# The low half of every fourth feed-forward weight group: ScalarE's negated high half and an accumulating transfer in place of VectorE's subtraction

## The reference

```python
hn = rmsnorm(x, norm_ffn_pre[l])
u = jnp.square(jax.nn.relu(jnp.einsum('bsd,df->bsf', hn, w_up[l])))     # w_up   2048 x 8192
y = jnp.einsum('bsf,fd->bsd', u, w_down[l])                             # w_down 8192 x 2048
x = x + rmsnorm(y, norm_ffn_post[l])
```

## Time and profile before

| | us |
|---|---|
| median of 3 runs | 2577.0 (2576.7 to 2577.39) |
| the profiled execution, its own time | 2578.93 |
| its span in the trace | 2577.2 |
| TensorE busy | 2571.3 (100%) |
| VectorE busy | 1582.6 (61%) |
| ScalarE busy | 1246.6 (48%) |
| GpSimd busy | 34.8 (1%) |

### The profile page before, as it was taken

The page is one execution under the profiler, slowest core; times in us unless marked ns, Lnnn a source line. Parts: engine busy times, 40 slices in busy tenths (PEclk is TensorE's granted clock), DMA queues, the critical chain, the costliest instruction groups (busy, mean ns, idle before and its releaser), DMA issues.

```text
span 2577.2 us, 29181 instructions
## 1 busy us (share of the span) xinstructions
PE 2571.3 (100%) x11503; PEld 2131.7 (83%) x11503; DVE 1582.6 (61%) x1842; ACT 1246.6 (48%) x1495; POOL 34.8 (1%) x56
## 2 busy tenths in 40 slices
PE   9999999999999999999999999999999999999999
PEld 7888888888888888888888888888888888888887
DVE  5646565566666566676866876556575555555555
ACT  6554443444555555455544444444464354454453
POOL 1000000000000000000000000000010000000000
PEclk9999999999999999999999999999999999999999
DMA  8767766676777777777565877666566676676674
GB/s 273 205 193 208 205 205 192 199 205 199 216 217 198 211 207 199 223 224 218 168 187 167 222 215 216 203 200 197 192 212 215 194 202 218 186 217 208 196 223 151
DMA packets 534793, 527.41 MB, mean 205 GB/s; under 512 B 294896, under 2 KB 297824, under 8 KB 534656
## 3 DMA queue, kind: packets, MB, share of 16 engines
q1 hardware_dynamic: 531856, 518.09, 67.5%
q0 software_dynamic: 2384, 6.93, 1.1%
q10 hardware_dynamic: 416, 0.52, 0.1%
HBM read 488.24 MB, written 2.10 MB: 190 GB/s over the span
## 4 chain that ended last, share of the span: by engine, by line
PE 99%; DMA 0%; DVE 0%; ACT 0%; issue 0%; SPq 0%
PE bank L1931 32%; PE bank L1933 32%; PE bank L1932 32%; PE bank L2080 1%; PE bank L2069 1%; PE bank L2059 1%; PE bank L2002 0%; DMA t_stage<-in_a_w_in_dram 0%; PE bank L2015 0%; PE bank L2008 0%; PE bank L2140 0%; PE bank L2127 0%; PE bank L1993 0%; PE bank L2160 0%; PE bank L2153 0%; PE bank L2208 0%
## 5 line engine op out<-in xcount | busy, mean ns | idle before, releaser
L1052 DVE TENSOR_TENSOR t_wl<-t_stage,t_wh 128x1024 fp32r<-128x1024 f32 x912 | 1105.5, 1221 | 818.7 <-ACT t_wh L561 816.7
L561 ACT ACTIVATE t_wh<-t_stage 128x1024 fp32r<-128x1024 f32 x913 | 957.2, 1057 | 969.3 <-PE bank L1933 962.4
L1931 PE MATMUL bank<-t_wl,t_xth 128*128 128x512 f32 x2480 | 972.1, 392 | 0.4 <-DVE t_xtl L1073 0.4
L1933 PE MATMUL bank<-t_wh,t_xtl 128*128 128x512 f32 x2480 | 965.2, 389 | 0.0
L1932 PE MATMUL bank<-t_wh,t_xth 128*128 128x512 f32 x2480 | 965.0, 389 | 0.0
L1931 PEld LDWEIGHTS bank<-t_wl,t_xth 128*128 128x128 f32 x2480 | 465.7, 188 | 96.7 <-DVE t_xtl L1073 0.9
L1933 PEld LDWEIGHTS bank<-t_wh,t_xtl 128*128 128x128 f32 x2480 | 465.5, 188 | 96.9
L1932 PEld LDWEIGHTS bank<-t_wh,t_xth 128*128 128x128 f32 x2480 | 465.7, 188 | 96.0 <-issue 0.2
L1931 PE MATMUL bank<-t_wl,t_yth 128*128 128x512 f32 x1026 | 399.2, 389 | 0.0
L1932 PE MATMUL bank<-t_wh,t_yth 128*128 128x512 f32 x1026 | 398.7, 389 | 0.0
L1933 PE MATMUL bank<-t_wh,t_ytl 128*128 128x512 f32 x1026 | 398.7, 389 | 0.0
(11 more groups left out here) (304 smaller groups left out, 946.0 us busy)
## 6 DMA issues: line engine op xcount, KB each, us to landing
t_stage<-in_a_w_in_dram SPq DMA_DIRECT2D x192, 512.0 KB, 4.2
t_stage<-in_w_in_dram SPq DMA_DIRECT2D x178, 512.0 KB, 4.3
t_stage<-in_b_w_in_dram SPq DMA_DIRECT2D x128, 512.0 KB, 4.5
t_stage<-in_w_up_dram SPq DMA_DIRECT2D x128, 512.0 KB, 3.9
t_stage<-in_w_down_dram SPq DMA_DIRECT2D x128, 512.0 KB, 4.3
t_stage<-in_a_w_out_dram SPq DMA_DIRECT2D x64, 512.0 KB, 4.1
t_ytl<-t_pool SPq DMA_DIRECT2D x128, 128.0 KB, 3.1
t_stage<-in_b_w_out_dram SPq DMA_DIRECT2D x32, 512.0 KB, 4.5
```

Source lines behind the costliest of these rows:

```text
L561: e.activation(wh[:, j % N_SPLIT], stage[:, j % N_STAGE], ACT.Copy).then_inc(*hi(j))
L1052: e.tensor_tensor(low, src, high.bitcast(F32), ALU.subtract).then_inc(*lo(j))
L1931: e.matmul(o, h, w_l, start=start, stop=False)
L1933: return e.matmul(o, l, w_h, start=False, stop=stop)
```

## The change

Of the groups 675, 679, 683 and so on to 895 (every fourth group, 56 in all; 675 is in chunk 2 of `up` of quarter 0), VectorE no longer makes the low half. In its place:

- ScalarE, right behind the copy `wh = stage`, waits for that copy of its own and writes `wl = -wh` (a second ACTIVATE of 128 x 1024).
- GpSimd waits for that and issues a transfer from `stage` to `wl` that adds (`accum_op=ALU.add`), so that `wl` becomes `stage - wh`. Before it, it waits for the landing of the second such transfer before.
- TensorE, before the group's first matmul, and SP, before the load that reuses the `stage` slot, wait for the landing of this transfer, where they waited for VectorE's instruction.

```diff
+    low_in = [signal(f"low_in{i}", 16) for i in range(2)]
...
+    sent_lows = [j for j in range(first["up", 0, 2] + 1, N - 16, 4)]
+
+    def low_done(j):
+        if j in sent_lows:
+            return low_in[sent_lows.index(j) % 2].at(j)
+        return lo.at(j)
...
                 if j >= N_STAGE:
-                    e.wait_ge(*lo.at(j - N_STAGE))
+                    e.wait_ge(*low_done(j - N_STAGE))
                 e.dma_start(wide(stage, j % N_STAGE, width), w[r:r + 128 * nk, c0:c0 + width].rearrange(
...
             load_row(c, A["norm_ffn_post_2"][:, cols(c)], "ffn", c)
+            for n, j in enumerate(sent_lows if c == 1 else ()):
+                e.wait_ge(*act.at("minus", j))
+                if n >= 2:
+                    e.wait_ge(*low_done(sent_lows[n - 2]))
+                e.dma_start(wl[:, j % N_SPLIT], stage[:, j % N_STAGE], accum_op=ALU.add).then_inc(*low_in[n % 2](j))
...
                 e.activation(wh[:, j % N_SPLIT], stage[:, j % N_STAGE], ACT.Copy).then_inc(*hi(j))
+                if j in sent_lows:
+                    e.wait_ge(*hi.at(j))
+                    e.activation(wl[:, j % N_SPLIT], wh[:, j % N_SPLIT].bitcast(F32), ACT.Copy,
+                                 scale=-1.0).then_inc(*act("minus", j))
...
                 j = count["lo"]
+                if j in sent_lows:
+                    count["lo"] += 1
+                    continue
...
-                e.wait_ge(*lo.at(j))
+                e.wait_ge(*low_done(j))
```

## The result

| | before | with the change |
|---|---|---|
| median | 2577.19 us (2576.7 to 2577.55, 4 runs) | 2646.77 us (2640.96 to 2651.16, 4 runs) |
| ratio | | 1.0268, 95% interval 1.0255 to 1.0281 |
| the profiled execution, its own time | 2578.93 us | 2644.35 us |
| its span | 2577.2 us | 2642.6 us |

A forecast was written before the change was run, and what follows sets the result against it. TensorE was taken to bound the kernel, so VectorE's freed 69 us were worth nothing. Stalls of 2.6 us at group 675 and 1.7 at four ends of `up` made 4.3, median 2581.3 us; range 2576.6 to 2625.

The forecast's parts named there:

- Step 1: At group 675, the first sent: low half at 1922.1 against 1919.46, so TensorE waits 2.6 us.
- X: Time of the accumulating transfer from GpSimd's issue to landing, taken as 5.9 us (4.2 with one reading, 8.0 at slowest).
- the second reading: In the transfer: the addition reads both operands, so its bytes count twice, 3.4 us of engine time instead of 1.7.
- the fixed part: In the transfer: issue and latency of 2.5 us, taken from a 3.4 us row load.
- Step 2: At the other 55 sent groups: transfer of 5.9 us is under 7.9 in `up` and 8.4 in `down`, no wait.
- The time left: What the transfer may take before TensorE needs the group: 7.9 us in `up`, 8.4 in `down`, 3.3 at group 675.
- Step 3: At the last chunk of each `up`: a transfer delays the sends, stall 0 to 0.9 us, 0.4 taken, 1.7 for four.
- Step 4: On GpSimd's queue: the third row load stands behind the 56 transfers, but is hidden; no cost.
- The clock: TensorE's granted clock: falling to 1.2 GHz for one group after 675's stall would cost 2.7 us; only widens the range.
- Late at every chunk's end: Rival: at 14 chunk ends of `up` sends meet a transfer, 1.5 us each, 21 us, 2601 in all; chance 0.13.
- Too slow everywhere: Rival: TensorE waits for the low half in all 56 groups, 2681 us, or bandwidth lengthens `up`, 2603; chance 0.17.

The follow-up runs named there:

- mid_down: The change with only `down`'s sent groups from its fourteenth group on (16 of the 56), still every fourth: 2577.03 us, ratio 0.9999.
- down_only: The change with only the 28 sent groups of `down`, still every fourth: 2596.3 us, ratio 1.0072.
- mid_kick: mid_down with one transfer in each of the first three quarters (703, 767, 831) pushed late once: 2587.36 us, ratio 1.0042.
- eighth_beside: The change with every eighth group (28), transfers issued together with a chunk's sends: 2581.59 us, ratio 1.0017.
- idle_transfer: The change with VectorE making all low halves; negations and 56 accumulating transfers remain, between spare buffers nobody waits for: 2601.42 us, ratio 1.0092.
- hold_only: idle_transfer, with SP's load into a sent group's slot also waiting for that group's idle transfer to land: 2645.56 us, ratio 1.0271.
- own_slots: The change with sent groups loaded into four buffers of their own, so no SP load waits for a transfer's landing: 2619.2 us, ratio 1.0164.
- eighth_clear: The change with every eighth group (27), transfers issued when a chunk's sends are out: 2577.57 us, ratio 1.0003.

## Why the prediction was wrong, by its own steps

**Step 1, group 675: right.** 2.6 us were forecast and 2.24 measured, with 4.5 us left behind the copy as forecast. GpSimd issued at 1914.50 and TensorE went on at 1919.88, so X was at most 5.4 us there (5.9 set).

**X alone: the second reading right, the fixed part too high.** The shortest transfer of the changed kernel lands after 4.4 us, those of the good stretch after 4.7, where 5.9 was set. A plain copy lands after 2.8 at best where the sum for one reading gave 4.2. So the 2.5 us of issue and latency, from the row load, were some 1.5 us too many. The second operand does cost what was set: 2.7 us of the engines against 1.5 for the copy. On this the Trainium skill (Collectives: The Full Stack, on why ReduceScatter is half of AllGather) and the run agree, a factor of 1.84 where it has two. The fit in the Trainium skill (DMA: Bandwidth & Descriptors, Anatomy of one DMA), an estimate of 3.2 us, does not agree with the 4.4.

**Step 2, the other 55 groups: this step failed.** It read "5.9 is under 7.9 and 8.4: no wait", with both sides as constants. In 26 of the 55 groups there was a wait, 34 us in all, and the clock and the restarts came on top. Both sides had moved.

*The time left.* The 7.9 us were read at group 687, which is copied behind a chunk's relu. The first sent group behind a `t_yth` is copied only when the sends have landed. Step 3 let the sends be late and asked only for `t_ytl`, not for the copies behind `t_yth` in ScalarE's program. At 691, where the same 7.9 to 8.4 us were taken for granted, the transfer had 3.9. The eleven such places behind 675 make 25 of the 34 us.

*X.* It was argued down with the words that the loads that would compete are themselves held back. They are held back, and then come all at once, ahead of the next transfer. I had worked out the release of one load (720, at 2025.8) and not asked what stands behind it on SP: the loads of the three groups after it. The terms of the loop were in the rows: four loads of 1.7 us of engine time, 3.4 of the transfer by the prediction's sum (2.7 measured) and its 2.5 of issue and latency. That is an estimate of 12.0 to 12.7 us against 10.88; the issues were 11.2 to 11.7 us apart. With X at 9.1 in the median there, the low half is late even with 8.4 us left. The runs show this part: the same groups are free in mid_down and late in down_only; at spacing five and eight there is no wait for a low half at all; with the last load behind the transfer 10.3 us of waits become 1.9; one push alone (mid_kick) dies out. In the changed kernel it is the smaller part by its waits.

**Step 3, the ends of `up`: right place, right size for one transfer.** 0 to 0.9 us each were forecast, and eighth_beside shows 0.9 at most, the upper end and not the 0.4 that I took. At spacing four the sends are also held behind the loads and lengthened on SP: 8.6 us in the changed kernel, and 15.0 in idle_transfer without any hold.

**Step 4, GpSimd's queue:** no wait of TensorE or VectorE for a row load appears.

**The clock** was only named as widening the range, at 2.7 us once. It was up to some 13 us, and the restarts behind the stalls, some 7 us by the estimate above, had no term at all.

**The rivals.** "Late at every chunk's end" named the collision but priced it without what it starts; that its 2601 is near idle_transfer's 2601.4 is chance. "Too slow everywhere" gave 2603 to 2681 and the result lies there, but by another mechanism: 27 groups late and not 56, X over 8 us only where loads stand ahead of it, and most of the wait where the time left had shrunk. The range stopped at 2625 because that case had 0.17.

What stays open: how the 70 us of the changed kernel split between hold and shared engines, and whether the large waits would go if the copies of the groups behind a `t_yth` stood ahead of it. idle_transfer lost 24 us and hold_only 68, own_slots 42; they do not add up, since each changes when the loads go out. Nor is it shown why a transfer from GpSimd starts only behind a burst of SP's loads in place of sharing the engines with it, as the prediction had it ("interleaves with the rest").

No version beat the kernel before. TensorE has nothing to gain here, and the best that these versions reach is its time, with 27 (eighth_clear) or 16 (mid_down) subtractions less on VectorE.

## What to carry to other kernels

When a wait for a VectorE instruction becomes a wait for a transfer, ask what the same wait holds on the loading queue, and follow the release: here all loads held went out together, and the next transfer stood behind them. Add up that loop and compare it with the compute time of the same groups. Read the time left at every kind of group, above all at those that an engine reaches only after another wait, such as ScalarE's copies behind `t_yth`: a latency that fits at one group says little about the next. And try a change in parts that do not meet: 27 of these transfers cost nothing measurable, 28 others 4.5 us, and the 56 together 70.

## What the runs showed of the hardware

- An accumulating transfer of 512 KB inside SBUF takes 2.7 us of all 16 DMA engines (a copy 1.5), lands 4.4 us after its issue at best and 10.5 at worst in the changed kernel. GpSimd is busy 0.86 us issuing it, where a plain copy of the same bytes took 0.53 and a row load 0.54.
- The issue of a 128 KB send on SP takes 0.62 us at least and up to 8.0 in the changed kernel, and what is behind it on SP waits; in idle_transfer four sends took 7.71 us to issue while the engines' share was 0.99 to 1.03:

```profile
L397 SPq DMA_DIRECT2D t_ytl<-t_pool x60: 615/940/8044, 1922.6 to 2556.0; - x60
```

- A stall of 2.24 us in a TensorE stream without gaps was followed by a stretch at 1.2 GHz. In the changed kernel so were stalls of 2.01, 2.77, 3.09, 3.25 and 3.39 us, but not those of 2.20, 2.21, 2.59 and 3.06 us: the length of the stall alone does not tell. down_only, with 16 waits of 2.1 us at most, kept a mean granted clock of 1.000.
